# A fused two-block transformer kernel: the heads' second half reordered, modulation rows copied by DMA, the shared expert woven into the routing

## What is computed

```python
# block 1
mod = silu(c) @ ada_w + ada_b                         # 6 x 1024 modulation values
sh1, sc1, g1, sh2, sc2, g2 = split(mod, 6)
h = rms_norm(x, norm1_g) * (1 + sc1) + sh1
z = h @ w_in
x = x + g1 * (concat(fox_mixer(z), rwkv7_mixer(z)) @ w_out)
h = rms_norm(x, norm2_g) * (1 + sc2) + sh2
x = x + g2 * moe_ffn(h, ...)
# moe_ffn: scores = sigmoid(h @ router_w); the best 4 of 8 groups, then the best 6 of 64 experts;
#          routed = sum of w_e * swiglu(h, expert e); shared = swiglu(h, shared weights)
# block 2: token mixer, cross attention, then
gate, up = split(rmsnorm(x, norm_ffn_pre) @ w_ffn_in, 2)   # 1024 x 5632
x = x + rmsnorm((silu(causal_conv3(gate) + b) * up) @ w_ffn_out, norm_ffn_post)
```

## Time and profile before

| | us |
|---|---|
| median of 3 runs | 1439.46 (1436.92 to 1439.6) |
| the profiled execution | 1441.09, span 1438.5 |
| PE busy | 1352.1 (94%) |
| DVE busy | 640.7 (45%) |
| ACT busy | 364.2 (25%) |
| POOL busy | 43.9 (3%) |
| TensorE clock, mean granted | 0.97 of full |
| moved by DMA | 339.10 MB, mean 236 GB/s |

### The profile page before, as it was taken

The page is one execution under the profiler, slowest core; times in us unless marked ns, Lnnn a source line. Parts: engine busy times, 40 slices in busy tenths (PEclk is TensorE's granted clock), DMA queues, the critical chain, the costliest instruction groups (busy, mean ns, idle before and its releaser), DMA issues.

```text
span 1438.5 us, 20229 instructions
## 1 busy us (share of the span) xinstructions
PE 1352.1 (94%) x8028; PEld 860.9 (60%) x8028; DVE 640.7 (45%) x1201; ACT 364.2 (25%) x624; POOL 43.9 (3%) x50
## 2 busy tenths in 40 slices
PE   5998988999889999999999999899999998999997
PEld 2535446875544444444444444568778566899985
DVE  2136357627632222222222222465347843777763
ACT  0202240020111222212212222245321112345542
POOL 0014200000000000000000000300000000000000
PEclk9999999969899999999999999999979999999999
DMA  9774275006529999999999997935530231355552
GB/s 340 238 231 144 73 300 228 3 1 242 236 97 400 419 420 415 416 420 406 415 418 421 414 416 290 312 132 160 163 27 21 97 118 59 117 177 191 190 178 85
DMA packets 94536, 339.10 MB, mean 236 GB/s; under 512 B 8736, under 2 KB 42168, under 8 KB 65677
## 3 DMA queue, kind: packets, MB, share of 16 engines
q1 hardware_dynamic: 84192, 319.06, 57.8%
q10 hardware_dynamic: 8109, 12.33, 3.5%
q0 software_dynamic: 2176, 6.86, 1.4%
HBM read 333.22 MB, written 1.05 MB: 232 GB/s over the span
## 4 chain that ended last, share of the span: by engine, by line
PE 82%; DVE 11%; DMA 3%; issue 2%; ACT 2%; ACTq 0%; DVEq 0%
PE bank L1847 16%; PE bank L1334 10%; PE bank L1863 8%; PE bank L1349 6%; PE bank L1350 6%; PE bank L1351 6%; PE bank L1810 3%; PE bank L1811 2%; PE bank L1828 2%; PE bank L1830 2%; DMA small<-in_norm_g 2%; PE bank L1320 2%; PE bank L1361 2%; DMA ring<-in_w_in 1%; PE bank L1747 1%
## 5 line engine op out<-in xcount | busy, mean ns | idle before, releaser
L1334 PE MATMUL bank<-ring,xT 128*128 128x512 f32 (+1 forms) x416 | 183.4, 598 | 7.1 <-DMA ring<-in_w_in 3.0
L1334 PEld LDWEIGHTS bank<-ring,xT 128*128 128x128 f32 x416 | 80.6, 196 | 97.8 <-issue 86.2
L1863 PE MATMUL bank<-dn,tmp 128*64 128x512 f32 x528 | 120.6, 598 | 0.0
L2924 DVE TENSOR_TENSOR xT<-bank,mod 128x512 fp32r<-128x512 f32 x66 | 45.7, 692 | 157.9 <-ACT mod L1084 150.7
L2917 DVE SCALAR_TENSOR_TENSOR tmp<-silu_c,rc,bank 128x256 f32<-128x256 f32 x33 | 22.6, 684 | 196.7 <-ACT silu_c L1071 191.4
L1349 PE MATMUL bank<-mod,w_high 128*128 128x256 f32 x352 | 98.6, 280 | 1.7 <-DVE xT L3424 1.7
L1350 PE MATMUL bank<-xT,w_high 128*128 128x256 f32 x352 | 98.6, 280 | 0.0
L1351 PE MATMUL bank<-mod,ring 128*128 128x256 f32 x352 | 98.2, 279 | 0.0
L3411 DVE TENSOR_TENSOR ring<-ring,w_high 128x1024 fp32r<-128x1024 f32 x66 | 77.8, 1221 | 22.0 <-ACT w_high L1269 20.3
L1320 PE MATMUL bank<-c_ident 128*128 128x128 f32 (+1 forms) x568 | 76.0, 285 | 0.0
L1863 PEld LDWEIGHTS bank<-dn,tmp 128*64 128x64 f32 x528 | 35.0, 136 | 68.3 <-issue 68.3
(11 more groups left out here) (653 smaller groups left out, 2311.9 us busy)
## 6 DMA issues: line engine op xcount, KB each, us to landing
dn<-in_exp_w_down SPq DMA_DIRECT2D x66, 1024.0 KB, 10.3
ring<-in_exp_w_gate SPq DMA_DIRECT2D x34, 1024.0 KB, 9.3
ring<-in_exp_w_up SPq DMA_DIRECT2D x34, 1024.0 KB, 11.4
...
```

Of the source, the lines that this page charges most:

```text
L1334: mm = pe.matmul(bank[lin_bank(o)][:, 0:n], lhs(k, t), ring[:, j % RING, k * n:(k + 1) * n], start=(k == 0), stop=(k == kt - 1 and not bias))
L1863: mm = pe.matmul(bank[6 + h][CHUNKS[c], :], act_eT[:, 0, k, CHUNKS[c]], dn[:, 2 * parity + c, lo:lo + BANK], start=(k == 0), stop=(k == D_ ...
L2924: dve.tensor_tensor(y_low[:, c], bank[6 + h][:, :], y_high[:, c].bitcast(F32), ALU.subtract)\
```

## The change

It touches six places.

1. Two more slots for late units. They lie where `mu` and `z_prev` are, and are free once POOL's last interpolation is done (`lerp_done` 4). Units now go round six slots.
2. The heads from the fifth on. `scores(6)` moves ahead of head 4. ACT takes both tiles' sigmoids, and the root before them, at head 3. DVE splits `keys_and_bonus` into `keys` (4 operations, early) and `bonus` (3, late). Late units stand between a head's transposes and its value products, in place of `keep_warm` there.
3. The solve. ACT's `rstd(fs)` moves behind `u_evac` 2, and the `keep_warm` counts change.
4. The eight row products and their copies go. SP issues 32 DMAs from the 32 equal rows to each quarter of the partitions, once the state product is done.
5. Routing. Tile 0's transposes are copied by ACT and its router product runs on its own. The shared gate and up product fills PE around tile 1's norm and the routing, and the shared down product fills the waits of the ranking. `top` handles both tiles in one operation where it can.
6. FFN. The first three units are multiplied as plain fp32 (`raw_unit`, 32 products of 128x128 each, by tiles), two of them before tile 1 is transposed. They are not split.

The diff, cut to its core:

```diff
-        LATE_SLOTS = 4
-        late_slot = [ring[:, s // 2, s % 2 * 2 * D:(s % 2 + 1) * 2 * D] for s in range(LATE_SLOTS)]
+        RING_SLOTS = ("ring 0 low", "ring 0 high", "ring 1 low", "ring 1 high")
+        EXTRA_SLOTS = ("extra 0", "extra 1")
+        late_order = (RING_SLOTS[0:2] + EXTRA_SLOTS + RING_SLOTS[2:4]) * 2 + RING_SLOTS
...
+        RAW_UNITS = 3
...
-                if u < LATE_SLOTS:
-                    sp.wait_ge(lin_mm, last_of(J_VR if u < LATE_SLOTS // 2 else J_G))
+                if u < 2:
+                    sp.wait_ge(lin_mm, last_of(J_VR))
+                elif u < 4:
+                    sp.wait_ge(lerp_done, 4)
+                elif u < 6:
+                    sp.wait_ge(lin_mm, last_of(J_G))
                 else:
-                    sp.wait_ge(late_used, u - LATE_SLOTS + 1)
-                sp.dma_start(late_slot[u % LATE_SLOTS],
+                    sp.wait_ge(late_used, late_last(u) + 1)
+                sp.dma_start(late_slot[late_order[u]],
                              A["ada_w"][k * P:(k + 1) * P, (batch + 1) * 2 * D:(batch + 2) * 2 * D])\
-                    .then_inc(ada_full[1 + u % LATE_SLOTS], 16)
...
+            sp.wait_ge(late_summed, 2)
+            sp.wait_ge(sc_mm, SC_STATE + 1)
+            for i in range(N_ROWS):
+                copies = late_rows[i // 4][i % 4 * 32:i % 4 * 32 + 32, :]
+                for q in range(0, P, 32):
+                    sp.dma_start(ROW_OF[i // 2][q:q + 32, i % 2 * BANK:(i % 2 + 1) * BANK], copies)\
+                        .then_inc(ada_rows, 16)
...
-                elif h in (3, 4):
-                    in_copy(J_G, h - 3)
-                    low_rank_sigmoids(h - 3)
-                    if h == 4:
-                        rstd(ws[:, 1, :], ws[:, 0, :])
-                elif h == 5:
-                    act.wait_ge(lin_evac, after(J_G, 1))
-                    act.activation(z_fox[:, :, 1536:2048], z_fox[:, :, 1536:2048], ACT.Sigmoid).then_inc(fox_sig, 1)
+                elif h == 3:
+                    rstd(ws[:, 1, :], ws[:, 0, :])
+                    in_copy(J_G, 0)
+                    for t in range(T):
+                        low_rank_sigmoids(t)
                 elif h >= 6:
+                    if h == 6:
+                        in_copy(J_G, 1)
                     decays(h - 6)
             act.wait_ge(sc_mm, SC_CUM[2] + 1)
             act.activation(ws[:, 2, 0:4], bank[6 + SC_CUM[2] % 2][:, 0:4], ACT.Exp).then_inc(rw_exp, 1)
-            rstd(fs[:, 6, 0:16], fs[:, 5, 0:16])
+            act.wait_ge(lin_evac, after(J_G, 1))
+            act.activation(z_fox[:, :, 1536:2048], z_fox[:, :, 1536:2048], ACT.Sigmoid).then_inc(fox_sig, 1)
             act.wait_ge(u_mm, 1)
...
+            rstd(fs[:, 6, 0:16], fs[:, 5, 0:16])
...
-            for i in range(N_ROWS):
-                act.wait_ge(lin_mm, after(("row", i)))
-                act.activation(ROW_OF[i // 2][:, i % 2 * BANK:(i % 2 + 1) * BANK],
-                               bank[lin_bank(outputs[(("row", i), 0)])][:, :], ACT.Copy).then_inc(lin_evac, 1)
...
+            for g in range(2):
+                act.wait_ge(tp_mm, TP_H2 + g + 1)
+                act.activation(xT[:, 4 * g:4 * g + 4, 0:P],
+                               bank[4 + (TP_H2 + g) % 2][:, :].rearrange("p (i c) -> p i c", i=4), ACT.Copy)\
+                    .then_inc(tp_evac, 1)
...
+                pe.wait_ge(prob_ready, h + 1)
+                transposes([(i * P, (i + 1) * P, P, pr_sb[:, h % 2, i * P:(i + 1) * P]) for i in range(3)])
                 if h >= 4:
                     late_units(2)
-                    keep_warm((12, 6, 0, 0)[h - 4], 2, W1 - HD, HD)
-                pe.wait_ge(prob_ready, h + 1)
-                transposes([(i * P, (i + 1) * P, P, pr_sb[:, h % 2, i * P:(i + 1) * P]) for i in range(3)])
-                keep_warm(4, 2, W1 - HD, HD)
+                else:
...
-                if h in (5, 6):
-                    if h == 6:
-                        late_units(2)
-                    decay_sums(h - 5)
-                elif h == 7:
-                    tile_decay()
 
             scores(0)
-            for h in range(HEADS):
-                if h + 1 < HEADS:
-                    scores(h + 1)
+            for h in range(5):
+                scores(h + 1)
+                if h == 4:
+                    scores(6)
                 beside_head(h)
                 attend(h)
+            scores(7)
+            decay_sums(0)
+            attend(5)
+            attend(6)
+            decay_sums(1)
+            attend(7)
+            tile_decay()
+            late_units(2)
 
...
+            keep_warm(2, 5)
...
-            keep_warm(4, 4)
+            keep_warm(6, 6)
...
-            keep_warm(4, 4)
+            keep_warm(3, 4)
             pe.wait_ge(u_evac, 4)
             solved(1, bank[0])
-            keep_warm(4, 4)
+            keep_warm(6, 4)
             pe.wait_ge(u_evac, 5)
             read_out(1, bank[3])
-            for i in range(N_ROWS):
-                o, r = outputs[(("row", i), 0)], slice(i % 4 * 32, i % 4 * 32 + 1)
-                pe.wait_ge(lin_evac, o - 1)
...
+            keep_warm(6, 6)
+            transpose_all(xn, layer=2, tiles=(0,))
+            pe.wait_ge(router_loaded, 48)
+            router_bank = score_bank()
+            keep_warm(6, 7)
+            pe.wait_ge(tp_evac, TP_H2 + 2)
+            router_tile(router_bank, 0)
+            pe.wait_ge(lin_evac, after(J_OUT + 1, 0))
+            pe.wait_ge(sh_full, 48)
+            shared_gate_up(0, 0, 4)
+            transpose_all(xn, layer=2, tiles=(1,))
+            shared_gate_up(0, 4, 6)
+            pe.wait_ge(tp_evac, TP_H2 + 4)
+            router_tile(router_bank, 1).then_inc(sc_mm, 1)
+            shared_gate_up(0, 6, KT)
             pe.wait_ge(lin_evac, after(J_OUT + 1, 1))
+            shared_gate_up(1, 0, KT)
             pe.wait_ge(sc_evac, SC_ROUTER + 1)
-
-
-            pe.wait_ge(sh_full, 48)
-            for t in range(T):
-                for k in range(KT):
-                    mm = pe.matmul(bank[4 + t][:, :], xTk(k, t), gate_up_of(sh_gu, k),
-                                   start=(k == 0), stop=(k == KT - 1))
-                mm.then_inc(gu_mm, 1)
-
+            shared_transposes(0)
...
-            keep_warm(12, 0)
+            shared_transposes(1)
+            shared_down(0, 1)
...
-            keep_warm(7, 0)
...
+            def raw_unit(u, t):
...
+                for half in range(2):
+                    lo = half * 2 * P + t * P
+                    for k in range(KT):
+                        mm = pe.matmul(ffn_bank(u)[:, lo:lo + P], of_unit(ring, u, k * 256 + half * P, P), xTk(k, t),
+                                       start=(k == 0), stop=(k == KT - 1), skip_group_check=True)
...
-            keep_warm(28, 6)
+            keep_warm(6, 6)
+            pe.wait_ge(tp_evac, TP_FF + 2)
+            raw_unit(0, 0)
+            raw_unit(1, 0)
             transpose_all(xn, layer=6, tiles=(1,))
-            keep_warm(8, 6)
-
-            for i in range(FF_JOBS):
+            raw_unit(2, 0)
+            pe.wait_ge(tp_evac, TP_FF + 4)
+            raw_unit(0, 1).then_inc(lin_mm, 1)
+            raw_unit(1, 1).then_inc(up_mm, 1)
+            raw_unit(2, 1).then_inc(lin_mm, 1)
+
+            for i in range(1, FF_JOBS):
...
-            def keys_and_bonus(t):
+            def keys(t):
...
+            masked_scores(6)
+            keys(0)
             dve.wait_ge(lin_mm, last_of(J_G))
             dve.tensor_copy(late_cols, small[:, KT:2 * KT].unsqueeze(2).broadcast_to([P, KT, 32])).then_inc(cb_ready, 1)
             prob_copy(4)
-            keys_and_bonus(0)
-            masked_scores(6)
+            keys(1)
+            masked_scores(7)
             prob_copy(5)
-            keys_and_bonus(1)
+            bonus(0)
             shifted_decay(0)
-            masked_scores(7)
             prob_copy(6)
             decayed(0)
+            bonus(1)
             prob_copy(7)
             shifted_decay(1)
             decayed(1)
...
+            dve.wait_ge(late_used, late_order.index(EXTRA_SLOTS[1], 6) + 1)
...
+            tp_n[0] += 2
...
+                link(dve.tensor_tensor(m, v, over(k - 1), ALU.is_gt))
+                link(dve.tensor_reduce(best8[:, :, 8:9], m, AX.X, ALU.add))
+                link(dve.tensor_scalar(best8[:, :, 8:9], best8[:, :, 8:9], -1.0, float(k), ALU.mult, ALU.add))
+                link(dve.tensor_tensor(e, v, over(k - 1), ALU.is_equal))
...
+            shared_act(0)
...
+            shared_act(1)
+            split_low_rows(0)
...
+            make_pick(0)
```

227 lines of the change are left out of this document (123 added, 104 removed).

## The result

The changed kernel takes 1383.61 us (median of 4 runs, 1380.80 to 1385.84), the kernel before 1439.53 (4 runs, 1436.92 to 1445.98). The ratio is 0.9618, 95% interval 0.9591 to 0.9644: 56 us less. The profiled execution took 1383.96, with a span of 1381.5.

The account below looks back on a forecast made before the run. PE, busy 94% of the span, was taken as the bound, with its idle, warm-keeping and slow stretches to win. From 1441.1, -12.2 - 7.0 - 12.1 - 16.2 - 5.5 = -53.0 gives 1388.1, plus 1 makes 1389 us; range 1382 to 1402.

Parts of the forecast that it names:

- margin: On the whole sum: 1 us added for stalls that nobody listed, from 1388.1 to 1389.
- Solve, -7.05: Solve: `u_evac` 1 comes early, state products end near 294.5 instead of 301.55; 1.1 us is wait, the rest clock.
- The other reading: Solve: the removed pause need not be what costs the clock, so the gain could be only 1 us.
- Rows and `w_out`, -12.1: Row products go, -9.6 us; first half of `w_out` regains clock, -2.5; the 32 copies cost nothing under 32 us.
- (d): Row copies: the 32 land one after another, the kernel turns slower, near 1590 us; chance 0.02.
- Routing, -16.2: End of `w_out` to first expert product: 43.0 us instead of 59.3, by woven down product, earlier router, shorter lists, clock.
- (c): Routing binds on DVE at every high price, FFN too: 1394.5 us; chance within the 0.70 shared with forecast and (b).
- FFN, -5.5: Start of the FFN: plain fp32 products fill 11 us of waiting, unit 3 starts 5.5 us earlier.
- Heads, -12.2: Heads: PE's waits for DVE go, DMA then bounds PE; set-up's transposes begin at 205.9 instead of 218.14 us.
- (b): Heads: DMA refills six slots no faster than four, gain 8 us, 1393; chance within the 0.70 shared with forecast and (c).
- Rival (a): Clock: one half-clock stretch stays or comes up, 6.7 us, 1396, chance 0.19; two, 1402, chance 0.07.

Follow-up runs that it names:

- 64 copies: The changed kernel with 64 row copies of half the size in place of 32, same bytes: 1395.4 us, ratio 0.9716 to the kernel before.
- few loads: The changed kernel with late modulation units 6 to 11 loading 64 of 2048 columns, so data differ: 22.9 us from `J_G` to the set-up's transposes, 1405.1 in all.

## Why the prediction was right, and where it was off

The forecast was 1389, the sum before its margin 1388.1; measured were 1383.6, inside the range.

**Solve, -7.05: right, with its cause.** -6.8 in the trace; the move undone costs 5.7 in the solve and done alone gives 7.8. The term said that 1.1 us of wait and the rest as clock would go, and took full clock as the likelier of two readings. The other reading leaned on the row at 185 us, after which PE ran at full clock in spite of 3.53 us of idle time. That row was an accident of one execution: the same pause, in the same order of operations, brought half clock in two other traces. The trace of before itself held a row against it, which the term left out: behind 2.48 us of idle time L1493 took 1.71 us, where it takes 1.02 at full clock. TensorE: Matmul & The Clock Gate, Part 1, of the Trainium skill says that activity releases the throttle. The pauses of 1.01 and 1.51 us ahead of the solve agree in that each was followed by half clock; the one of 3.53 us in the trace of before was not. No rule that I could read from these rows says when a pause does it.

**Rows and `w_out`, -12.1: right in size, wrong in its slack.** -12.0 in the trace, and undone it costs 13.5, more clock included. `y_ready` didn't bind. The price of a copy was bounded from 12 transfers that land in 7.5 to 16.0 us. The slack was put at 32 us, up to DVE's first residual, which is 1.0 us per copy, and the point from which the kernel turns slower at 2.7. By the trace they have 27.4 us, since DVE waits for all of them ahead of `mod`, and use 21.5 in issue alone. The last of the 64 copies landed 1.4 us behind its issue, so copies cost from some 0.8 us each on (an estimate: 27.4 less 1.4, over 32). The right question was how fast SP issues them, 0.67 us each. The 64 copies show how near the mechanism of (d) was.

**Routing, -16.2: right as a sum.** -16.3. The marks came as replayed: ranking at + 25.1 (25.8), gather at + 36.5 (36.4), first expert product at + 42.9 (43.0). DVE's routing took 9.3 us, near the 10 of my list and not the 12.4 of the old pitch, so (c) fell. Of the parts, the down product undone costs 6.2 as it ran and 4.5 at full clock, where I had 5.4, and DVE's shorter lists 4.1 to 4.9. The rest, some 5 to 8 us for the earlier router and the clock, is argued and was not tried alone. The replay had PE arrive at + 25.8, inside its range for DVE (+ 24 to + 26.4). In the trace PE comes last to the ranking, by 2.2 us; 1.6 of it could be had, by moving a down product and two warm fills behind the ranking.

**FFN, -5.5: right.** -5.5 in the trace, 5.5 undone.

**Heads, -12.2: the size was off, and so was the rival.** The stretch behind `J_G` shrank by 11.3, not 12.9. The step that failed is the time of the loads: from `J_G`'s end to the batch that waits last, at 202.32, it is 23.6 us, where I had 1.6 + 8 x 2.55 = 22.0. The price of a unit was not too low: from 181 us on 423 GB/s were moved, 2.48 us for a unit. But in the 23.6 us 394 GB/s were moved, start included, which is 8.9 units and not 8. Part of it belonged to loads behind the eighth. Why they went ahead of its last part stays open. PE's own work, which I had at + 21.6 at full clock, takes 22.9 with few loads, 1.8 of it for two batches at half clock. So DMA bound the stretch, as the term said, by 1.8 us. (b) asked whether six slots are refilled faster than four. They are: 2.48 us a unit in place of 3.1. The two extra slots are worth 6.3 us (30.9 with four), but only in the new order: in the old one PE's waits for DVE are the bound and the slots are worth nothing. The gain against an average run of the kernel before is larger than 11.3, since its heads lose 6.5 us to the clock in some executions.

**What nobody priced: 3.5 us ahead of `J_G`.** No instruction differs there but `scores(6)`. The end of the last `J_G` tile lay between 175.1 and 182.2 us in fourteen traces, and in one of the kernel before with a single operation moved much later it was 178.6. So it is chance, as far as one trace for each kernel shows: the trace of before was the slowest of them. The two traces differ by 0.6 us at the end of the projections before the heads, by 1.9 through DVE's wait for POOL (below), and by 1.5 through a half clock near 136 us. The -1.4 in the loop is of this kind too: that stretch took 812.1 to 815.8 in the kernels that leave it alone. The levels' + 0.9 are pauses of PE with "issue" as their cause, of 0.2 to 1.1 us, at other places in each kernel; their cause stays open.

So of the 5.4 us by which the forecast was too high, 1 is the margin and about 6 lie in stretches that no edit touches but for `scores(6)` (4.2 ahead of `J_G`, 1.4 in the loop, 0.4 at the end): the chance in the one trace to which the sum was tied. Heads and levels took 1.6 + 0.9 of it back. That these two partly cancel, and that the sum came out so near, is luck. **Rival (a)** came only in small. It asked for a stretch that costs 6.7 us. What came is the stretch at 196 us, 1.4 us long in its effect and in front of a wait for a load. The sum had full clock there. It is no accident: all eleven traces with the new order of the heads show half clock between 192 and 204 us, behind short waits of PE for loads or for DVE (0.68 and 0.29 us in the changed kernel).

One reading of the earlier trace rows was wrong and did no harm: the third dip of the clock before, put near 1151 us, is the stretch from 1043 to 1079.
